# A two-layer hybrid encoder on one core: the residual stream kept with features on partitions, and the output projection turned to match

## The chip, the cores and the metric

The kernel runs on one core of a Trainium2 chip. The metric is the device time of one execution in microseconds; for the kernel before it is 845.27 us, the median of 3 runs (844.89 to 845.55). The profile is that of one execution.

## What is computed

Input x is 256 tokens by 2048 features in float32. Each of two layers normalises x, projects it to all branch inputs, runs four token mixers (retention, gated linear attention, pooling, latent attention), gates them, and adds the output projection to x:

```python
for l in range(DEPTH):                       # DEPTH = 2
    h = _rmsnorm(x, norm_g[l])               # x * rsqrt(mean(x*x) + EPS) * g
    z = h @ w_in[l]
    ...                                      # split z; y_a, y_b, y_c, y_d of the four mixers
    y = jnp.concatenate([y_a, y_b, y_c, y_d], axis=-1)
    x = x + y @ w_out[l]
```

## The kernel before

**Weights as a stream of granules.** All large weights of a layer come as 136 granules of 128 x 1024 float32 (512 KB), two blocks of 128 input rows by 512 output columns each. SyncE loads them into a ring of four buffers `raw` (L319). Each is split in two parts whose sum is the float32 value: ScalarE writes `hi` (L713), VectorE (in each layer POOL for the first three, L1358) writes `lo = raw - hi` (L978). TensorE multiplies hi by hi, lo by hi and hi by lo. The plan is fixed: stage mq has 8 granules (0 to 7), then lat (352 columns wide), and so on to rg (96 to 103) and the output stages out0 to out3 (104 to 135). A buffer is free for `hi` when its granule is `multiplied`, and for `raw` when it is `split`.

**Products.** In every stage of the stream the activations, x or y, are the stationary operand, 128 features by 128 tokens, and the weights are the moving one, 512 columns (L357). A granule is 2 blocks x 2 token halves x 3 products = 12 matmuls. Results go to one of two pairs of PSUM banks, `pair[0]` and `pair[1]`, which alternate from stage to stage; the four others, `bank[0..3]`, serve the mixers. `taken` says that a pair's result has been read. Gates such as rg are read out of their pair by `take` on ScalarE (L731).

**x and its turning.** x lies with tokens on partitions, `x[128, 2, 2048]`. At the start of a layer `turn_x(f)` transposes two feature tiles of x (four 128 x 128 transposes on TensorE, L388) into a bank; ScalarE rounds them with the norm's gain to `xT_hi` (L747) and VectorE writes `xT_lo` (L995). TensorE's order is turn_x(0), turn_x(1), granule 0, turn_x(2), granule 1, and so on. mq alone does the four hi-by-hi products of a granule first, and waits for the low parts behind them. The squares for the norm are taken on ScalarE with a sum over the row (L758); the factor `x_rs` is made by VectorE and POOL and applied when a stage is taken.

**Output.** In out0 to out3, VectorE adds each 128 x 512 result to x (L1325), the first half of the tokens when `half_out` says so, the second when the granule is done. The signals `added[c]` release the next layer's transposes and, in the last layer, SyncE's stores (L324).

**Order.** Every engine's order is written out by hand: `splits(n)` on ScalarE and VectorE and `granules(n)` on TensorE go on to granule n. The body of a layer stands once, in a loop (`Fori`) on each engine, and a wait's number is worked out from the layer register. What VectorE and TensorE do next to the end of a layer is thus the loop's branch back. The first loads are x's first quarter (SyncE), the identity, the gains and x's second quarter (ScalarE), and, after POOL's memsets, the last two quarters of x and the constants (L1344, L1346).

Of the kernel before, what the change touches and what calls it, by code (L numbers as in the profile page):

```python
# [17 lines left out]
F32 = mybir.dt.float32  # L18
# [6 lines left out]
P = 128  # L25
# [31 lines left out]
for i_ in range(4):  # L57
# [7 lines left out]
    ("mq", "lat", "mg", "pv", "pg", "gqk", "gv", "gg", "rq", "rk", "rv", "rg", "out0", "out1", "out2", "out3"))}  # L65
# [3 lines left out]
for n_, count_ in ORDER:  # L69
    w_, t_, b_, k_, per_ = STAGES[n_]  # L70
    if n_ not in done_:
        done_[n_], NTH[n_] = 0, used_[PAIR[n_]]
        used_[PAIR[n_]] += 1
# [40 lines left out]
def build(nc, x_in, stream, mats_in, gains_in, consts_in, out):  # L114
    with ExitStack() as ctx:
# [86 lines left out]
        x_sq = stats(MT * 4).rearrange("p (m c) -> p m c", m=MT)  # L202
# [29 lines left out]
        added = [signal(f"added{c}", MT, primed=1) for c in range(4)]  # L232
        gains_ready = signal("gains_ready", 1)
        half_out = signal("half_out", 4)
        act_step = signal("act_step", 4)
        dve_step = signal("dve_step", 24)
        tabs_ready = signal("tabs_ready", 6)
        x_filled, xT_rounded, xT_ready = signal("x_filled", 8), signal("xT_rounded", KT), signal("xT_ready", KT)
        x_squared, x_ms_ready, x_rs_ready = signal("x_squared", 8), signal("x_ms_ready", 1), signal("x_rs_ready", 1)
# [70 lines left out]
        def _(sp):  # L310

            sp.dma_start(x[:, :, 0:512], x_in.rearrange("(m p) (c n) -> c p m n", p=P, c=4)[0]
                         ).then_inc(x_loaded[0].sem, 16)
# [7 lines left out]
            for c in range(4):  # L321
                for m in range(MT):
                    sp.wait_ge(*added[c].at(DEPTH - 1, m + 1))
                    sp.dma_start(out.rearrange("(m p) (c n) -> m c p n", p=P, c=4)[m, c],  # L324
                                 x[:, m, c * 512:(c + 1) * 512]).then_inc(stored.sem, 16)
            sp.wait_ge(stored.sem, 16 * 4 * MT)
# [3 lines left out]
        def _(pe):  # L330
# [5 lines left out]
            with pe.Fori(0, DEPTH) as l:  # L336
                pos = [0]

                def granules(upto):

                    for j in range(pos[0], upto):
                        name, slots = PLAN[j]
                        width, src, base, n_slots, per = STAGES[name]
                        a, r = PAIR[name], j % RING
                        first = slots[0] == base
                        if first:
                            pe.wait_ge(*taken[a].at(l, MT * NTH[name]))
                        if name == "wq0" and first:
                            pe.wait_ge(*lqT_ready.at(l, 4))
# [1146 lines left out]
```

## Time and profile before

| | |
|---|---|
| median of 3 runs | 845.27 us (844.89 to 845.55) |
| profiled execution, first to last instruction (span) | 843.8 us |
| TensorE busy | 829.3 us (98%) |
| VectorE / ScalarE / POOL busy | 464.5 / 428.4 / 50.2 us |
| matmuls of the weight stream | 3 x 768 on x, 3 x 304 on y |
| mean granted TensorE clock | 0.996 |
| data moved | 150.67 MB, 179 GB/s |

The page gives for the profiled execution only its span; the time of a run is taken around the program, and its median is 1.5 us above the span. An engine that is 98% busy sets the time, so the profile is read for TensorE's own instructions, for its idle time and for what ended it. A matmul's recorded duration (0.39 us for 512 columns) is longer than the distance between two starts, because matmuls overlap; the distance is what counts. The granted clock is given as a share of 2.4 GHz.

### The profile page before, as it was taken

The page shows a single profiled execution, that of the slowest core. Times are in us where ns is not written, and L with a number is a line of the kernel's source. Part 1 is how long each engine was busy: PE and PEld are TensorE (multiplying, and loading weights), DVE is VectorE, ACT ScalarE, POOL GpSimd, SP SyncE. Part 2 cuts the span into 40 slices and gives each one's busy share as a digit, 9 for nine tenths or more (in the row PEclk, how much of TensorE's full clock was granted, in tenths as well). Part 3 has the DMA queues.
Part 4 walks back from the last instruction along what each step waited for, and adds up shares of the span by engine and source line. Part 5 has one row for each costly group of instructions (what it writes and reads, how often), then busy time and mean ns, then how long its engine had stood idle before and what let it go on. Part 6 is the DMA issues. An engine that isn't in the chain of part 4 may idle for free.

```text
span 843.8 us, 11480 instructions
## 1 busy us (share of the span) xinstructions
PE 829.3 (98%) x4084; PEld 701.4 (83%) x4084; DVE 464.5 (55%) x611; ACT 428.4 (51%) x616; POOL 50.2 (6%) x44
## 2 busy tenths in 40 slices
PE   6999999999999999999989999999999999999998
PEld 5898888888888888888869888888878888888886
DVE  2554497445375853654445635864653649546542
ACT  4864565456725543433347655663475345444441
POOL 6110000000000101000122000000000010010000
PEclk9999999999999999999989999999999999999999
DMA  8765764533543454565436656644354345546654
GB/s 343 251 230 190 240 215 150 174 125 126 175 150 125 147 178 150 193 206 198 156 117 227 246 186 227 198 150 150 125 175 147 128 147 162 176 139 204 194 186 140
DMA packets 41924, 150.67 MB, mean 179 GB/s; under 512 B 4752, under 2 KB 4880, under 8 KB 41744
## 3 DMA queue, kind: packets, MB, share of 16 engines
q1 hardware_dynamic: 40592, 145.25, 51.5%
q0 software_dynamic: 432, 2.88, 0.8%
q10 hardware_dynamic: 848, 1.83, 0.7%
q8 instruction: 34, 0.56, 0.3%
q14 instruction: 18, 0.15, 0.1%
HBM read 147.85 MB, written 2.10 MB: 178 GB/s over the span
## 4 chain that ended last, share of the span: by engine, by line
PE 96%; ACT 1%; issue 1%; DMA 1%; DVE 1%; SPq 0%; ACTq 0%; DVEq 0%
PE pair L357 84%; PE bank L388 4%; PE bank L637 1%; PE bank L611 1%; PE bank L500 1%; PE bank L679 1%; PE bank L669 1%; PE bank L592 1%; DMA raw<-stream 1%; PE bank L627 0%; PE bank L548 0%; PE bank L570 0%; PE bank L560 0%; ACT gate L731 0%; DVE lo L978 0%
## 5 line engine op out<-in xcount | busy, mean ns | idle before, releaser
L978 DVE TENSOR_TENSOR lo<-raw,hi 128x1024 fp32r<-128x1024 f32 (+3 forms) x266 | 307.3, 1178 | 213.1 <-ACT hi L713 209.2
L713 ACT ACTIVATE hi<-raw 128x1024 fp32r<-128x1024 f32 (+3 forms) x272 | 270.4, 1022 | 155.7 <-PE pair L357 132.5
L357 PE MATMUL pair<-lo,xT_hi 128*128 128x512 f32 (+1 forms) x768 | 296.9, 387 | 2.4 <-DVE xT_lo L995 2.4
L357 PE MATMUL pair<-hi,xT_hi 128*128 128x512 f32 (+1 forms) x768 | 296.0, 396 | 2.9 <-ACT xT_hi L747 2.6
L357 PE MATMUL pair<-hi,xT_lo 128*128 128x512 f32 (+1 forms) x768 | 296.9, 387 | 0.0
L357 PEld LDWEIGHTS pair<-lo,xT_hi 128*128 128x128 f32 x768 | 145.5, 189 | 30.2 <-issue 3.3
L357 PEld LDWEIGHTS pair<-hi,xT_hi 128*128 128x128 f32 x768 | 144.3, 189 | 30.4 <-ACT xT_hi L747 3.3
L357 PEld LDWEIGHTS pair<-hi,xT_lo 128*128 128x128 f32 x768 | 145.2, 189 | 28.5
L357 PE MATMUL pair<-hi,yT_hi 128*128 128x512 f32 (+1 forms) x304 | 116.7, 384 | 0.0
L357 PE MATMUL pair<-hi,yT_lo 128*128 128x512 f32 (+1 forms) x304 | 116.6, 383 | 0.0
L357 PE MATMUL pair<-lo,yT_hi 128*128 128x512 f32 (+1 forms) x304 | 116.5, 383 | 0.0
L357 PEld LDWEIGHTS pair<-lo,yT_hi 128*128 128x128 f32 x304 | 57.1, 188 | 10.8
L357 PEld LDWEIGHTS pair<-hi,yT_hi 128*128 128x128 f32 x304 | 57.1, 188 | 10.7
L357 PEld LDWEIGHTS pair<-hi,yT_lo 128*128 128x128 f32 x304 | 57.1, 188 | 10.6
L731 ACT ACTIVATE work<-pair,stat 128x512 f32<-128x512 f32 (+2 forms) x44 | 26.4, 653 | 47.0 <-PE pair L357 25.6
L1352 POOL TENSOR_TENSOR stat<-stat 128x2 f32<-128x2 f32 (+1 forms) x10 | 19.1, 1911 | 495.9 <-DVE stat L1001 495.9
L747 ACT ACTIVATE yT_hi<-bank,gains 128x256 fp32r<-128x256 f32 x44 | 17.4, 475 | 52.7 <-PE bank L388 52.7
L995 DVE SCALAR_TENSOR_TENSOR yT_lo<-bank,gains,yT_hi 128x256 fp32r<-128x256 f32 x44 | 18.3, 477 | 29.3 <-ACT yT_hi L747 29.3
L1325 DVE TENSOR_TENSOR x<-pair,x 128x512 f32<-128x512 f32 x16 | 11.1, 692 | 28.4 <-PE pair L357 28.4
L995 DVE SCALAR_TENSOR_TENSOR xT_lo<-bank,gains,xT_hi 128x256 fp32r<-128x256 f32 x32 | 13.9, 478 | 19.7 <-ACT xT_hi L747 19.7
L747 ACT ACTIVATE xT_hi<-bank,gains 128x256 fp32r<-128x256 f32 x32 | 13.3, 469 | 16.7 <-PE bank L388 16.7
L1245 DVE TENSOR_REDUCE stat<-work 128x4 f32<-128x512 f32 x8 | 5.5, 686 | 28.3 <-ACT work L931 15.1
(138 smaller groups left out, 519.7 us busy)
## 6 DMA issues: line engine op xcount, KB each, us to landing
raw<-stream SPq DMA_DIRECT2D x272, 512.0 KB, 4.2
out<-x SPq DMA_DIRECT2D x8, 256.0 KB, 5.3
consts<-consts_in POOLq DMA_DIRECT2D x1, 1792.0 KB, 14.9
mats<-mats_in ACTq DMA_DIRECT2D x2, 576.0 KB, 3.5
x<-x_in POOLq DMA_DIRECT2D x2, 512.0 KB, 9.3
x<-x_in SPq DMA_DIRECT2D x1, 512.0 KB, 4.6
x<-x_in ACTq DMA_DIRECT2D x1, 512.0 KB, 9.0
consts<-consts_in ACTq DMA_DIRECT2D x1, 64.0 KB, 4.3
```

The source lines that it names most:

```text
L357: return nc.tensor.matmul(pair[a][m][:, 0:width], x_part[:, slots[i], m * P:(m + 1) * P], w_part[r][:, i * 512:i * 512 + width], start=(sl ...
L388: t = nc.tensor.transpose(bank[b][:, i * P:(i + 1) * P], tile, ident)
L500: mm = nc.tensor.matmul(bank[m][:, h * HD:(h + 1) * HD], probsT[:, h % 2, j, m * P:(m + 1) * P], kv_sb[:, j, h, NOPE:NOPE + HD], start=(h ...
L592: mm = nc.tensor.matmul(bank[(2 + 2 * m + d) % 4][:, f * SEQ:(f + 1) * SEQ], e_neg[:, d, f, m * P:(m + 1) * P], q_heads[:, d, f, m].rearra ...
L611: mm = nc.tensor.matmul(bank[(2 + 2 * m + d) % 4][:, h * HD:(h + 1) * HD], k_dec[:, d, h], v_b[:, m, h * HD:(h + 1) * HD], start=True, sto ...
L713: nc.scalar.activation(cut[0], cut[1], ACT.Copy).then_inc(rounded[r].sem, 1)
L731: nc.scalar.activation(dst(m), pair[a][m][:, 0:cols], func, scale=rs[:, m:m + 1]).then_inc(ready.sem, 1)
L747: nc.scalar.activation(dst[:, slot0 + kt, :], bank[(b0 + f) % 4][:, i * SEQ:(i + 1) * SEQ], ACT.Copy, scale=gains[:, gain + kt:gain + kt + ...
L978: nc.vector.tensor_tensor(cut[0], cut[1], cut[2].bitcast(F32), ALU.subtract).then_inc(split[r].sem, 1)
L995: nc.vector.scalar_tensor_tensor(out=dst_lo[:, slot0 + kt, :], in0=bank[(b0 + f) % 4][:, i * SEQ:(i + 1) * SEQ], scalar=gains[:, gain + kt ...
L1325: nc.vector.tensor_tensor(at, pair[PAIR[f"out{c}"]][m][:], at, ALU.add).then_inc(added[c].sem, 1)
L1352: pool.tensor_tensor(rs, ms, minus_half[:, 0:n], ALU.pow).then_inc(rs_ready.sem, 1)
```

## The change

- x enters, stays and leaves with features on partitions, `xT[128, 16, 256]`; the host turns it. The transposes of x (`turn_x`) are gone. ScalarE makes xT_hi and VectorE xT_lo straight from xT in SBUF.
- In out0 to out3 the weights become the stationary operand, four tiles of 128 output columns per block, and y the moving one. y's high and low parts lie side by side in `yT[:, slot]` (2 x 256), so that one matmul of 512 columns gives weights-hi by y-hi and by y-lo, in the two halves of a bank; a second of 256 columns adds weights-lo by y-hi to the first half. Each output quarter uses four banks: the two pairs for out0 and out2, `bank[0..3]` for out1 and out3.
- VectorE adds both halves to xT, two dependent adds of 256 columns per tile. Before the adds of the last quarter of the first layer it makes the next layer's first eight tiles of xT_lo.
- The squares for the norm are now summed over partitions: ScalarE squares 1024 columns at a time into gate0 and gate1, POOL folds them into `x_sum[128, 256]`, and TensorE multiplies x_sum by a column of -0.5 ahead of mq's last granule.
- The loop over layers is written out on all engines but SyncE. POOL issues its x loads ahead of the memsets; ScalarE loads gains, x's second quarter and then the identity.

```diff
--- before.py
+++ after.py
-        yT_hi = sb("yT_hi", [P, KT, SEQ], F32R)
-        yT_lo = sb("yT_lo", [P, KT, SEQ], F32R)
-        x = sb("x", [P, MT, D_MODEL])
+        yT = sb("yT", [P, KT, 2, SEQ], F32R)
+        yT_hi, yT_lo = yT[:, :, 0, :], yT[:, :, 1, :]
+        xT = sb("xT", [P, KT, SEQ])
+        x_sum = sb("x_sum", [P, SEQ])
...
-            with pe.Fori(0, DEPTH) as l:
+            for l in range(DEPTH):
...
+                def out_granule(j, c, slots, first):
+                    r = j % RING
+                    pe.wait_ge(*split[r].at(l, j // RING + 1))
+                    if c == 0 and slots[0] % GT == 0:
+                        pe.wait_ge(*(yTD_ready, yTC_ready, yTB_ready, yTA_ready)[slots[0] // GT].at(l, 4))
+                    for t in range(4):
+                        into = pair[t // 2][t % 2] if c % 2 == 0 else bank[t]
+                        if first and c == 0 and t % 2 == 0:
+                            pe.wait_ge(*taken[t // 2].at(l, MT * PAIR_USES[t // 2]))
...
+                        if first and c >= 2:
+                            pe.wait_ge(*added.at(l, 4 * (c - 2) + t + 1))
+                        for i, slot in enumerate(slots):
+                            at = slice(i * 512 + t * P, i * 512 + (t + 1) * P)
+                            nc.tensor.matmul(into[:], hi[r][:, at], yT[:, slot].rearrange("p a t -> p (a t)"),
+                                             start=slot == 0, stop=False)
+                            mm = nc.tensor.matmul(into[:, 0:SEQ], lo[r][:, at], yT[:, slot, 0, :],
+                                                  start=False, stop=slot == KT - 1)
+                        if slots[-1] == KT - 1 and t < 3:
+                            mm.then_inc(tile_out.sem, 1)
+                    mm.then_inc(multiplied[r].sem, 1)
...
-                for f in range(8):
...
-                    turn_x(f)
-                    if f >= 1:
-                        granules(f)
+                granules(7)
+                pe.wait_ge(*x_summed.at(l, 4))
+                pe.wait_ge(*added.at(l, 0))
+                pe.wait_ge(cleared.sem, 1)
+                for m in range(MT):
+                    mm = nc.tensor.matmul(bank[2][:, 2 * m:2 * m + 2], x_sum[:, m * P:(m + 1) * P], minus_half[:, 0:2],
+                                          start=True, stop=True)
+                mm.then_inc(ms_filled.sem, 1)
                 granules(13)
...
+                def lo_x(l, f):
+                    dve.wait_ge(*xT_rounded.at(l, 2 * f + 2))
+                    for kt in (2 * f, 2 * f + 1):
+                        nc.vector.scalar_tensor_tensor(
+                            out=xT_lo[:, kt, :], in0=xT[:, kt, :], scalar=gains[:, G_NORM + kt:G_NORM + kt + 1],
+                            in1=xT_hi[:, kt, :].bitcast(F32), op0=ALU.mult, op1=ALU.subtract).then_inc(xT_ready.sem, 1)
...
                 for c in range(4):
                     splits(min(114 + 8 * c, GRANULES))
-                    j = END[f"out{c}"] - 1
-                    dve.wait_ge(*half_out.at(l, c + 1))
-                    for m in range(MT):
...
+                    if c == 3 and l + 1 < DEPTH:
+                        for f in range(4):
+                            lo_x(l + 1, f)
+                    for t in range(4):
...
+                        nc.vector.tensor_tensor(at, into[:, 0:SEQ], at, ALU.add).then_inc(half_added.sem, 1)
+                        dve.wait_ge(*half_added.at(l, 4 * c + t + 1))
+                        nc.vector.tensor_tensor(at, into[:, SEQ:2 * SEQ], at, ALU.add).then_inc(added.sem, 1)
...
+            for c in range(2, 4):
+                pool.dma_start(xT[:, 4 * c:4 * c + 4, :], x_in[c]).then_inc(x_loaded[c].sem, 16)
             pool.memset(minus_half, -0.5).then_inc(cleared.sem, 1)
...
+                for c in range(4):
+                    sq = (gate0, gate1)[c % 2][:].rearrange("p m c -> p (m c)")
+                    pool.wait_ge(*x_squared.at(l, c + 1))
+                    pool.tensor_tensor(sq[:, 0:512], sq[:, 0:512], sq[:, 512:1024], ALU.add).then_inc(x_folded.sem, 1)
...
```

**TensorE at the start of a layer.** The rows name the line, the operation, the tile written and those read, and the waits. Before:

```order
L406 ISA [waits x_loaded0,yA_ready]
L388 MATMUL bank<-consts,x 128x128 [waits added0]
L388 MATMUL bank<-consts,x 128x128 x7
L347 ISA
L365 ISA [waits taken0]
L366 ISA [waits rounded0]
L357 MATMUL pair<-hi,xT_hi 128x512 [waits xT_rounded]
L357 MATMUL pair<-hi,xT_hi 128x512 x3
L370 REGISTER_ALU [waits xT_ready]
L357 MATMUL pair<-lo,xT_hi 128x512 [waits split0]
```

After, from the last two matmuls of the first layer on:

```order
L363 MATMUL bank<-yT,hi 128x512
L365 MATMUL bank<-yT,lo 128x256
L392 MATMUL pair<-hi,xT_hi 128x512 [waits rounded0,xT_rounded,added,taken0]
L392 MATMUL pair<-hi,xT_hi 128x512 x3
L392 MATMUL pair<-lo,xT_hi 128x512 [waits split0,xT_ready]
```

The eight transposes between out3 and mq are gone, with the waits of the turned tiles, and mq follows out3 directly.

**TensorE in the first output granule.** Before:

```order
L370 REGISTER_ALU [waits yTD_ready,taken0]
L357 MATMUL pair<-hi,yT_hi 128x512 [waits split0]
L357 MATMUL pair<-lo,yT_hi 128x512
L357 MATMUL pair<-hi,yT_lo 128x512
L357 MATMUL pair<-hi,yT_hi 128x512
L357 MATMUL pair<-lo,yT_hi 128x512
```

After:

```order
L363 MATMUL pair<-yT,hi 128x512 [waits taken0,yTD_ready,split0]
L365 MATMUL pair<-yT,lo 128x256
L363 MATMUL pair<-yT,hi 128x512
L365 MATMUL pair<-yT,lo 128x256
L363 MATMUL pair<-yT,hi 128x512
L365 MATMUL pair<-yT,lo 128x256
L363 MATMUL pair<-yT,hi 128x512
L365 MATMUL pair<-yT,lo 128x256
L363 MATMUL pair<-yT,hi 128x512 [waits taken1]
```

Wide and narrow matmuls alternate, and from the third tile on the granule needs the second pair of banks too, which before was not needed until out1.

**VectorE at the last output quarter of the first layer.** Before:

```order
L978 TENSOR_TENSOR lo<-raw,hi 128x1024 [waits rounded3]
L1325 TENSOR_TENSOR x<-pair,x 128x512 [waits half_out]
L1323 REGISTER_ALU
L1325 TENSOR_TENSOR x<-pair,x 128x512 [waits multiplied3]
L968 REGISTER_ALU [waits added3]
L968 COMPARE_AND_BRANCH
```

After:

```order
L1004 TENSOR_TENSOR lo<-raw,hi 128x1024 [waits rounded3]
L1033 SCALAR_TENSOR_TENSOR xT_lo<-xT,gains,xT_hi 128x256 [waits xT_rounded]
L1033 SCALAR_TENSOR_TENSOR xT_lo<-xT,gains,xT_hi 128x256
...
L1367 TENSOR_TENSOR xT<-bank,xT 128x256 [waits tile_out]
L1369 TENSOR_TENSOR xT<-bank,xT 128x256 [waits half_added]
...
L1367 TENSOR_TENSOR xT<-bank,xT 128x256 [waits multiplied3]
L1369 TENSOR_TENSOR xT<-bank,xT 128x256 [waits half_added]
L1004 TENSOR_TENSOR lo<-raw,hi 128x1024 [waits rounded3,gains_ready]
```

The next layer's first xT_lo tiles stand ahead of the adds, and its first split of VectorE behind them.

## Rows read from the trace of the kernel before

**Rows 1.** The page's head and busy times of the engines.
```profile
span 843.8 us, 11480 instructions
PE 829.3 (98%) x4084; PEld 701.4 (83%) x4084; DVE 464.5 (55%) x611; ACT 428.4 (51%) x616; POOL 50.2 (6%) x44
```
**Rows 2.** Waits of TensorE: whom it waited for, us in total, times, longest.
```profile
PE bank L388 <- DMA x<-x_in: 5.6, 1, 5.6
PE pair L357 <- ACT xT_hi L747: 2.6, 2, 2.1
PE pair L357 <- DVE xT_lo L995: 2.4, 1, 2.4
```
**Rows 3.** Timeline of TensorE, change of layers: start, us, operation, idle before.
```profile
422.05 0.39 PE L357 MATMUL pair<-hi,yT_lo 128*128 128x512 f32 x1
...
423.96 1.19 PE L357 MATMUL pair<-hi,xT_hi 128*128 128x512 f32 x4 [0.49 <-ACT xT_hi L747]
427.51 0.79 PE L357 MATMUL pair<-lo,xT_hi 128*128 128x512 f32 x1 [2.36 <-DVE xT_lo L995]
...
454.24 0.32 PE L357 MATMUL pair<-hi,xT_hi 128*128 128x352 f32 x1
```
**Rows 4.** ScalarE and VectorE there; last, a window's busy times, clock, DMA share, GB/s.
```profile
423.07 0.84 ACT L747 ACTIVATE xT_hi<-bank,gains 128x256 fp32r<-128x256 f32 x2 [5.13 <-PE bank L388]
426.50 1.66 DVE L995 SCALAR_TENSOR_TENSOR xT_lo<-bank,gains,xT_hi 128x256 fp32r<-128x256 f32 x4 [3.33 <-ACT xT_hi L747]
427.50:433.00 5.50, 5.49 (x15) 4.42 (x16) 0.66 (x2) 0.82 (x3) 2.11 (x1) 0.50 0.56 191
```
**Rows 5.** Timeline of TensorE at the start of the first layer.
```profile
14.49 0.60 PE L388 MATMUL bank<-consts,x 128*128 128x128 f32 x4
14.84 1.17 PE L357 MATMUL pair<-hi,xT_hi 128*128 128x512 f32 x4
...
33.70 1.07 PE L357 MATMUL pair<-hi,xT_hi 128*128 128x512 f32 x4
36.42 0.32 PE L357 MATMUL pair<-hi,xT_hi 128*128 128x352 f32 x1
```
**Rows 6.** POOL and ScalarE at the start, and a window with its DMA rate.
```profile
4.03 1.67 POOL L1344 DMA_DIRECT2D x<-x_in x2
7.87 1.06 ACT L713 ACTIVATE hi<-raw 128x1024 fp32r<-128x1024 f32 x1 [3.78 <-DMA raw<-stream]
9.01 2.36 POOL L1358 TENSOR_TENSOR lo<-raw,hi 128x1024 fp32r<-128x1024 f32 x1 [2.74 <-ACT hi L713]
6.00:8.00 2.00, 1.58 (x8) 1.17 (x6) 0.00 (x0) 0.13 (x1) 0.27 (x1) 1.00 1.01 359
```
**Rows 7.** TensorE in the attention scores and out stage, and the page's weight loads.
```profile
138.54 0.28 PE L472 MATMUL bank<-yT_lo,yT_hi 128*128 128x256 f32 x1
140.10 0.28 PE L477 MATMUL bank<-yT_lo,yT_hi 128*128 128x256 f32 x1
391.90 0.39 PE L357 MATMUL pair<-lo,yT_hi 128*128 128x512 f32 x1
398.70 0.39 PE L357 MATMUL pair<-lo,yT_hi 128*128 128x512 f32 x1
L357 PEld LDWEIGHTS pair<-lo,yT_hi 128*128 128x128 f32 x304 | 57.1, 188 | 10.8
```
**Rows 8.** Timeline of TensorE and ScalarE where out0 begins.
```profile
334.33 0.39 PE L357 MATMUL pair<-hi,yT_hi 128*128 128x512 f32 x1
334.53 1.27 ACT L731 ACTIVATE gate<-pair,stat 128x512 f32<-128x512 f32 x2 [2.97 <-PE pair L357]
```
**Rows 9.** End of the program, and VectorE's cost for 256 columns from PSUM.
```profile
839.91 0.39 PE L357 MATMUL pair<-hi,yT_lo 128*128 128x512 f32 x1
840.34 0.69 DVE L1325 TENSOR_TENSOR x<-pair,x 128x512 f32<-128x512 f32 x1 [0.67 <-PE pair L357]
L995 DVE SCALAR_TENSOR_TENSOR xT_lo<-bank,gains,xT_hi 128x256 fp32r<-128x256 f32 x32 | 13.9, 478 | 19.7 <-ACT xT_hi L747 19.7
```

More of the change, by code:

```diff
@@ L64 @@
 PAIR = {n_: i_ % 2 for i_, n_ in enumerate(
[L65 removed]
+    ("mq", "lat", "mg", "pv", "pg", "gqk", "gv", "gg", "rq", "rk", "rv", "rg"))}
 PAIR.update({n_: 0 for n_ in ("wq0", "wq1", "wkv0", "wkv1")})
@@ L321, in _ @@
             for c in range(4):
-                for m in range(MT):
[L323 to L326, printed above, removed]
+                sp.wait_ge(*added.at(DEPTH - 1, 4 * c + (4 if c < 3 else 1)))
+                n = 4 if c < 3 else 1
+                sp.dma_start(out[c, :, 0:n], xT[:, 4 * c:4 * c + n, :]).then_inc(stored.sem, 16)
+            for j in range(1, 4):
+                sp.wait_ge(*added.at(DEPTH - 1, KT - 4 + j + 1))
+                sp.dma_start(out[3, :, j:j + 1], xT[:, KT - 4 + j:KT - 3 + j, :]).then_inc(stored.sem, 16)
+            sp.wait_ge(stored.sem, 16 * 7)
         @block.tensor
@@ L343, in granules @@
                         width, src, base, n_slots, per = STAGES[name]
+                        first = slots[0] == base
+                        if name.startswith("out"):
+                            out_granule(j, int(name[3:]), slots, first)
+                            continue
                         a, r = PAIR[name], j % RING
-                        first = slots[0] == base
                         if first:
                             pe.wait_ge(*taken[a].at(l, MT * NTH[name]))
+                        if first and name in ("mq", "lat"):
+                            pe.wait_ge(*added.at(l, (10 if name == "mq" else 12) - KT))
                         if name == "wq0" and first:
@@ L371, in granules @@
                         ends = slots[-1] == base + n_slots - 1
-                        if name.startswith("out") and ends:
-                            each.sort(key=lambda im: im[1])
                         for i, m in each:
@@ L378, in granules @@
                             mm = product(i, m, t_lo, hi, last=ends and i == per - 1)
-                            if name.startswith("out") and ends and (i, m) == (per - 1, 0):
-                                mm.then_inc(half_out.sem, 1)
                         mm.then_inc(multiplied[r].sem, 1)
@@ L962, in _ @@
         def _(dve):
-            for sig in (*split, *added, yA_ready, yTA_ready, la_ready, score_b_ready):
+            for sig in (*split, yA_ready, yTA_ready, la_ready, score_b_ready):
                 dve.sem_inc(sig.sem, 1)
+            dve.sem_inc(added.sem, KT)
             dve.wait_ge(gains_loaded.sem, 16)
             nc.vector.tensor_copy(gains[:], gains_all[:, 0:GAIN_W]).then_inc(gains_ready.sem, 1)
-            with dve.Fori(0, DEPTH) as l:
+            for l in range(DEPTH):
                 pos, step = [POOL_SPLITS], [0]
```

136 lines of the change are left out of this document (68 added, 68 removed).

## The prediction

> **What bounds the kernel now.** I read the page's busy shares first: TensorE is busy 829.3 of a span of 843.8 us, VectorE and ScalarE about half of it [rows 1]. So only what TensorE executes, and what it waits for, counts. Its waits come to under 11 us, and all of the long ones are in the stretch in which x is turned and rounded: 5.6 for the first part of x, 2.6 for xT_hi, 2.4 for xT_lo [rows 2]. The timeline then says where. At the change of layers the last output matmul is issued at 422.05, the transposes follow, TensorE waits 0.49 for ScalarE, does four matmuls, waits 2.36 for VectorE, and the stage behind (lat, the first of 352 columns) begins only at 454.24 [rows 3]. VectorE's idle time of 3.33 us ends long after its input is there (xT_hi is written from 423.07 on, 0.84 us for both tiles; VectorE starts at 426.50; I take this for the branch back of its loop, since nothing else stands there), and after TensorE's wait the granted clock is 0.50, the lower of its two levels (1.2 of 2.4 GHz) [rows 4]. Everything else is a steady stream: in the output stage 30 matmuls of 512 columns start in 6.80 us, 226.7 ns each [rows 7]. The sum below is made against the profiled span of 843.8 us; the median of the runs, 845.27 us, is 1.5 above it, and I carry the difference over unchanged.
>
> **Out stage, more matmuls: +3.4 us.** A granule was 12 matmuls of 512 columns, 12 x 0.2267 = 2.72 us. It becomes 8 of 512 and 8 of 256: the same 6144 columns, but four more instructions and weight loads. The only 256-column matmuls of the same data type stand in the attention scores: 13 intervals in 1.56 us, 120 ns each, every one with its own weight load [rows 7]. 8 x 0.2267 + 8 x 0.120 = 2.774, so +0.053 per granule, and 64 granules give +3.4. Lower end: two narrow ones cost what a wide one did, 113 ns each, so nothing is added: 0. What the row doesn't show is a narrow matmul between wide ones; that is a rival below. The Trainium skill (TensorE: Matmul & The Clock Gate, section "Packing small matmuls", what overlaps) says that a weight load overlaps a running matmul only in another row group, and gives a load of 128 columns as 107 ns ("LDWEIGHTS"). By that rule this change's 4 x 64 = 256 extra loads would add 27 us instead of 3.4. A whole 256-column matmul with its load stands every 120 ns, so the trace speaks against it.
>
> **Change of layers: -9.9 us.** Before, from the end of the last output matmul (422.05 + 0.23 = 422.28) to the first lat matmul (454.24) pass 31.96 us [rows 3]. In that stretch lie 8 granules of mq, 8 x 2.72 = 21.8; the rest is 32 transposes, the waits and matmuls at half clock. After the change the transposes are gone, the loop is written out, and mq's first six granules need features 0 to 1535, whose sums are complete one quarter earlier; VectorE makes the low parts of the first eight feature tiles before it adds the last quarter. Tiles 12 to 15 are needed 6 x 2.72 = 16 us after the last output matmul, and their 8 adds take 4 us. What is late next is the norm: squares on ScalarE, three folds per quarter on POOL, then a matmul ahead of mq's last granule (19 us after). POOL takes 2.36 us for 1024 columns [rows 6], so one quarter's folds of 512, 256 and 256 are 2.4 us; ScalarE's last square waits behind a split that needs granule 3 multiplied (11 us), so the sum is there at 11 + 1.1 + 1.1 + 2.4 + latencies, some 16 us: hidden, with 3 to spare. The two matmuls of 2 columns themselves I put at 0.3 us (4 transposes take 14.84 - 14.49 = 0.35 us [rows 5]; ends 0.2 and 0.6). 31.96 - 21.8 - 0.3 = 9.9 saved, ends 9.3 and 10.1.
>
> **Start: -0.5 us, the least certain term.** Before, the first lat matmul is at 36.42. Granule 0 is done when the transposes at 14.49 begin, and mq's last granule, 7, starts at 33.70: 19.2 us for six granules, which need 6 x 2.72 = 16.3. So the six sets of transposes between them cost 2.9 [rows 5]. Granule 0 itself is bound by its low part: weights landed and ScalarE at 7.87, POOL from 9.01 to 11.37 [rows 6], which no transpose delays. So the best case is -2.9 + 0.3 = -2.6. Against it stands the order of loads. POOL now issues its two x transfers (1 MB) ahead of its memsets instead of at 4.03 [rows 6], and ident, for which TensorE waits at its very start, is queued on ScalarE behind 0.5 MB of x. The DMA engines are full there, 359 GB/s from 6 to 8 us [rows 6], so 1 MB ahead of the first weights is up to 2.8 us. Then POOL's three splits of 2.4 us follow one another, and only VectorE's, from granule 3 on, catch up; the end of this case is +1.5. I take half of the delay, so most of the gain is spent: -0.5. The Trainium skill (DMA: Bandwidth & Descriptors, "Queues, rings and completion order", arbitration) says that each engine goes round its queues packet by packet. By it the weights would get a third while three queues have work, and the first granule would land about 2 us later; that would put this term near zero.
>
> **Handover of rg: +0.7 us.** The first output granule now writes all four pair banks. Two of them hold rg, which ScalarE takes from 334.53 to 335.80 and releases near 336.05; the granule starts at 334.33 [rows 8] and reaches the third tile after 8 of 16 matmuls, 1.39 us later, at 335.72. So TensorE waits 0.35 in each layer, 0.7 in all (ends 0 and 1.0).
>
> **End: +1.1 us.** Before, VectorE's last add (0.69) starts at 840.34, 0.2 after the last matmul's slot (839.91 + 0.23) [rows 9]. Now each 128x256 tile is two chained adds. The nearest row is 0.48 for 256 columns out of PSUM [rows 9]; half the 512-wide add is 0.35; I take 0.43. A tile with its waits is near 1 us, TensorE makes one in 0.69, so VectorE falls behind and ends 2.0 after the last matmul instead of 0.9: +1.1, ends 0.7 and 2.0. The same backlog stands at the other quarters: VectorE is 2 us late with the next split, which is due 5.5 us after the quarter's end, so it costs nothing; if it did, TensorE would show waits on lo in each quarter.
>
> The unrolled loop adds no instruction that is executed and removes register work; outside the change of layers the rows show no cost for it, so zero. The new load order of yT and the adds of lo_x out of SBUF lie on ScalarE and VectorE, half idle: zero.
>
> **Sum:** 3.4 - 9.9 - 0.5 + 0.7 + 1.1 = -5.2, so 845.27 - 5.2 = 840.1 us.
>
> **Rivals.**
> 1. *The narrow matmul exposes its weight load* (slower). A weight load is recorded with 188 ns [rows 7]. If a narrow matmul behind a wide one held TensorE for its load's 188 instead of 120, 512 x 0.068 = 35 us: 875 us. There are 512 narrow matmuls, so the gain of 5.2 is gone from 130 ns each, and from 134 on it is slower by over 0.2%. For it: no row has this mixture. Against: 120 ns in the scores. The Trainium skill's rule on weight loads (TensorE: Matmul & The Clock Gate, as above) points the same way as this rival, with less. 8%.
> 2. *The sum of squares comes late.* If POOL's folds or their semaphores take twice what I say, TensorE waits about 2 us in each layer ahead of granule 7: 844 us. Against it: 3 us of slack at the change of layers; for it, about 1 us at the start. 8%.
> 3. *The start is fast:* the loads keep their order of arrival, -2.6 instead of -0.5, and VectorE's adds cost what half a wide one does: 837.6. 15%.
> 4. *The low clock stays.* A new wait at the start or at the layers keeps TensorE at the lower level for some 6 us, as after 427.51; 3 us are given back: 843. 6%.
> 5. *The adds at each quarter starve the ring,* 1 us in each of 6 quarters: 846, no difference. 5%.
>
> **Numbers.** My forecast, 839 to 842, has 58%. The range takes in rivals 2 to 4: 836.6 to 844.0; outside are rivals 1 and 5 and a little of the fast side. A measurement of this kernel can tell 0.2%, 1.7 us, from nothing. Faster: the forecast, 3, 4 and a part of 2, about 0.82; within 0.2%: rival 5 and the rest of 2, 0.10; slower: rival 1, 0.08.
>
> **What would show it.** The output stage at 2.77 us per granule, narrow matmuls every 120 ns. From the last output matmul of the first layer to the first lat matmul 22.1 us, no wait of TensorE over 0.3 there, granted clock at the upper level throughout, no transposes of x. A wait near 0.35 for ScalarE in the first output granule. The first lat matmul at 36 and the last add some 2 us behind TensorE's last. I am wrong if narrow matmuls stand 130 ns apart or more, if TensorE waits for x_sum, or if the first lat matmul comes after 38.

## The result, and the profile after

The changed kernel takes 846.03 us (median of 20 runs, 845.78 to 846.35); the kernel before, on the same chip, 844.92 (20 runs; one of them, at 1045.8 us, was slow and is left out of the ratio). The ratio is 1.0017, with a 95% interval of 1.0010 to 1.0024. Forecast were 840.1 and a range of 836.6 to 844.0, so the prediction was wrong: about 5 us of gain were expected, and 1.1 us of loss came.

The page of the changed kernel, its head and the busy rows, and VectorE's row of xT_lo:

```profile
span 844.4 us, 11528 instructions
PE 824.6 (98%) x4284; PEld 705.0 (83%) x4284; DVE 499.5 (59%) x657; ACT 425.0 (50%) x590; POOL 75.0 (9%) x66
...
L1033 DVE SCALAR_TENSOR_TENSOR xT_lo<-xT,gains,xT_hi 128x256 fp32r<-128x256 f32 x32 | 32.9, 1069 | 11.0 <-ACT xT_hi L776 11.0
```

TensorE is busy 4.7 us less than before [rows 1], in a span that is 0.6 longer, so it waits more. And one instruction of VectorE, same shape, has gone from 478 [rows 9] to 1069 ns. The waits of TensorE after the change (whom it waited for, us in total, times, longest):

```profile
PE pair L392 <- ACT hi L733: 10.9, 1, 10.9
PE pair L392 <- DVE lo L1004: 3.7, 5, 1.0
PE pair L392 <- POOL lo L1397: 1.1, 2, 0.8
```

The waits for xT_hi and xT_lo [rows 2] are gone. In their place stand a longer start and waits of 1 us for lo, the low part of the weights. The timeline of TensorE says where (start, us, operation, idle before):

```profile
10.95 2.05 PE L392 MATMUL pair<-hi,xT_hi 128*128 128x512 f32 x4 [10.95 <-ACT hi L733]
...
30.38 1.07 PE L392 MATMUL pair<-hi,xT_hi 128*128 128x512 f32 x4
32.48 0.47 PE L392 MATMUL pair<-lo,xT_hi 128*128 128x512 f32 x1 [1.03 <-DVE lo L1004]
34.38 1.07 PE L392 MATMUL pair<-hi,xT_hi 128*128 128x512 f32 x4
...
41.61 0.32 PE L392 MATMUL pair<-hi,xT_hi 128*128 128x352 f32 x1
...
429.49 0.28 PE L365 MATMUL bank<-yT,lo 128*128 128x256 f32 x1
429.60 1.09 PE L392 MATMUL pair<-hi,xT_hi 128*128 128x512 f32 x4
...
449.57 0.50 PE L428 MATMUL bank<-stat,x_sum 128*128 128x2 f32 x4
...
452.78 0.32 PE L392 MATMUL pair<-hi,xT_hi 128*128 128x352 f32 x1
```

The first lat matmul comes at 41.61 instead of 36.42 [rows 5]. The granules of mq follow one another every 4.0 us (30.38 to 34.38) where 2.72 was reckoned. The change of layers, in contrast, is nearly a stream without a wait (the longest is 0.2 us): out3's last matmul is issued at 429.49, lat begins 23.29 us later, where 32.19 passed before [rows 3].

Four points in time divide the span of every kernel of this study: the first matmul of out0 in layer 1, the issue of the last output matmul of layer 1, the first lat matmul of layer 2, and the end of the span. All are read from TensorE's timeline:

```
kernel                        start to out0   out stage   to lat of layer 2   rest     span
before                            334.33        87.72           32.19        389.56   843.8
after                             339.38        90.11           23.29        391.62   844.4
  difference                       +5.05        +2.39           -8.90         +2.06    +0.6
before, loop written out          333.83        87.72           26.70        389.15   837.4
```

The last line is the fourth experiment's. It shows what the prediction had not separated: 5.5 of the 8.9 us at the change of layers are got without the change of layout. The +2.06 of the rest is the second layer's out stage, 90.10 us (750.55 to 840.65) where 87.72 passed before, less 0.3 in other places.

VectorE in the first layer after the change:

```profile
6.65 0.88 DVE L1033 SCALAR_TENSOR_TENSOR xT_lo<-xT,gains,xT_hi 128x256 fp32r<-128x256 f32 x2 [1.05 <-ACT xT_hi L776]
11.49 2.36 DVE L1033 SCALAR_TENSOR_TENSOR xT_lo<-xT,gains,xT_hi 128x256 fp32r<-128x256 f32 x2 [3.96 <-ACT xT_hi L776]
...
30.58 1.76 DVE L1004 TENSOR_TENSOR lo<-raw,hi 128x1024 fp32r<-128x1024 f32 x1
32.26 2.39 DVE L1033 SCALAR_TENSOR_TENSOR xT_lo<-xT,gains,xT_hi 128x256 fp32r<-128x256 f32 x2
34.57 1.75 DVE L1004 TENSOR_TENSOR lo<-raw,hi 128x1024 fp32r<-128x1024 f32 x1
36.25 0.87 DVE L1033 SCALAR_TENSOR_TENSOR xT_lo<-xT,gains,xT_hi 128x256 fp32r<-128x256 f32 x2
```

VectorE at the change of layers, after:

```profile
426.21 7.04 DVE L1033 SCALAR_TENSOR_TENSOR xT_lo<-xT,gains,xT_hi 128x256 fp32r<-128x256 f32 x4 [0.37 <-ACT xT_hi L776]
```

And POOL in the first layer:

```profile
10.81 2.37 POOL L1397 TENSOR_TENSOR lo<-raw,hi 128x1024 fp32r<-128x1024 f32 x1 [4.40 <-ACT hi L733]
...
20.89 1.48 POOL L1402 TENSOR_TENSOR gate<-gate 128x512 f32<-128x512 f32 x1
...
31.21 2.27 POOL L1402 TENSOR_TENSOR gate<-gate 128x512 f32<-128x512 f32 x1
33.56 0.81 POOL L1407 TENSOR_TENSOR gate<-gate 128x256 f32<-128x256 f32 x1
34.45 0.79 POOL L1411 TENSOR_TENSOR x_sum<-x_sum,gate 128x256 f32<-128x256 f32 x1
```

Two xT_lo tiles take 0.88 us while POOL is idle (6.65; 36.25, just after its last fold of x at 35.24) and about 2.4 while it splits or folds; a split of VectorE takes 1.75 instead of the 1.23 it had before. POOL's fold of 512 columns takes 1.48 beside xT_lo (20.89) and 2.27 where a split of VectorE runs with it (31.21); POOL's own splits keep 2.4 us beside xT_lo. One mq granule needs one split and two xT_lo from VectorE, 1.76 + 2.39 less some overlap: the 4.0 us of TensorE's granules.

ScalarE's first two roundings show the second cause, the loads:

```profile
9.60 1.06 ACT L733 ACTIVATE hi<-raw 128x1024 fp32r<-128x1024 f32 x1 [3.06 <-DMA raw<-stream]
...
13.58 1.06 ACT L733 ACTIVATE hi<-raw 128x1024 fp32r<-128x1024 f32 x1 [2.12 <-DMA raw<-stream]
```

Before, the first weights were there at 7.87 [rows 6]. So two theories stood after this reading, for the +5.05: A, the order of the first loads delays the weights; B, VectorE and POOL slow each other down, now that VectorE reads xT_lo's operands, x and xT_hi, both from SBUF, where it used to read x from PSUM.

### The profile page after: what moved, and what is told of

Same layout as the page of the kernel before. It is cut to its first block, busy times and chain, and to the rows that moved or that the text cites. A ratio compares the mean times of both kernels' runs of the same rounds, so it can differ in the third digit from the quotient of the medians.

```text
span 844.4 us, 11528 instructions
## 1 busy us (share of the span) xinstructions
PE 824.6 (98%) x4284; PEld 705.0 (83%) x4284; DVE 499.5 (59%) x657; ACT 425.0 (50%) x590; POOL 75.0 (9%) x66
## 4 chain that ended last, share of the span: by engine, by line
PE 91%; DVE 5%; DMA 2%; ACT 1%; issue 1%; SPq 0%; ACTq 0%
PE pair L392 59%; PE pair L363 7%; PE bank L363 6%; PE pair L365 3%; PE bank L365 3%; PE bank L419 3%; DVE xT_lo L1033 3%; DVE lo L1004 2%; DMA raw<-stream 2%; PE bank L658 1%; PE bank L632 1%; PE bank L700 1%; PE bank L521 1%; PE bank L613 1%; PE bank L690 1%
## 5 line engine op out<-in xcount | busy, mean ns | idle before, releaser
L363 PE MATMUL pair<-yT,hi 128*128 128x512 f32 x256 | 90.0, 395 | 0.1
L363 PE MATMUL bank<-yT,hi 128*128 128x512 f32 x256 | 88.9, 391 | 0.0
L365 PE MATMUL pair<-yT,lo 128*128 128x256 f32 x256 | 71.7, 280 | 0.0
L365 PE MATMUL bank<-yT,lo 128*128 128x256 f32 x256 | 71.7, 280 | 0.0
L363 PEld LDWEIGHTS pair<-yT,hi 128*128 128x128 f32 x256 | 48.0, 187 | 11.6 <-ACTq L756 0.8
L363 PEld LDWEIGHTS bank<-yT,hi 128*128 128x128 f32 x256 | 47.9, 187 | 10.5
L365 PEld LDWEIGHTS pair<-yT,lo 128*128 128x128 f32 x256 | 48.4, 189 | 0.1
L365 PEld LDWEIGHTS bank<-yT,lo 128*128 128x128 f32 x256 | 48.4, 189 | 0.0
L1033 DVE SCALAR_TENSOR_TENSOR xT_lo<-xT,gains,xT_hi 128x256 fp32r<-128x256 f32 x32 | 32.9, 1069 | 11.0 <-ACT xT_hi L776 11.0
L392 PE MATMUL pair<-hi,yT 128*128 128x384 f32 (+1 forms) x96 | 27.5, 353 | 0.0
```

The source lines that it names most:

```text
L363: nc.tensor.matmul(into[:], hi[r][:, at], yT[:, slot].rearrange("p a t -> p (a t)"), start=slot == 0, stop=False)
L365: mm = nc.tensor.matmul(into[:, 0:SEQ], lo[r][:, at], yT[:, slot, 0, :], start=False, stop=slot == KT - 1)
L392: return nc.tensor.matmul(pair[a][m][:, 0:width], x_part[:, slots[i], m * P:(m + 1) * P], w_part[r][:, i * 512:i * 512 + width], start=(sl ...
L1033: nc.vector.scalar_tensor_tensor(out=xT_lo[:, kt, :], in0=xT[:, kt, :], scalar=gains[:, G_NORM + kt:G_NORM + kt + 1], in1=xT_hi[:, kt, :]. ...
```

## The experiments

Every kernel ran beside the kernel before on the same chip; the ratios are to it.

### 1 to 3: the loads, the folds, and both

In e1 the first loads are issued in the order of before:

```diff
 act:
+    act.dma_start(const("ident"), consts_in[:, 0:P])
     act.dma_start(gains_all[:], gains_in)
     act.dma_start(xT[:, 4:8, :], x_in[1])
-    act.dma_start(const("ident"), consts_in[:, 0:P])
 pool:   (the two x loads)
-    ahead of the memsets
+    behind the memsets
```

In e2 POOL's folds of the squares shrink to two columns each, so most of the mean square of x is left out:

```diff
-pool.tensor_tensor(sq[:, 0:512], sq[:, 0:512], sq[:, 512:1024], ALU.add)
+pool.tensor_tensor(sq[:, 0:2], sq[:, 0:2], sq[:, 512:514], ALU.add)
```

(the other folds in the same way, but for the first of 256 columns in each layer). e3 has both edits.

Expected of e1:

> The changed kernel with the first loads issued as before (POOL's x loads behind its memsets, ScalarE: identity, gains, x). Theory A, the loads alone made the start late (weights of granule 0 landed at 9.6 instead of 7.9 us): the first lat matmul comes back from 41.6 to about 36, the time falls by 5 us to 841. Theory B, VectorE's xT_lo out of SBUF (two operands in SBUF, 1.2 us instead of 0.44 while POOL folds the squares) made it late: the time falls by 1 us at most. I expect both to count: first lat matmul near 39.5, 844 us.

Of e2:

> The changed kernel with POOL's folds cut to 2 columns (only one 256-column add per layer is kept), so the norm's sum leaves out most of the squares. Theory A (loads): start unchanged, 846. Theory B (POOL beside VectorE): xT_lo tiles behind granule 2 take 0.44 us each again, the splits 1.23 instead of 1.76; the first lat matmul comes near 38.5, 843 us; the 3 tiles made beside POOL's own splits stay slow.

Of e3:

> Both edits: loads issued as before, and POOL's folds cut to 2 columns (the norm's sum leaves out most squares). If A and B are all of it, the start is as the prediction had it: first lat matmul at 34.5 to 36, 839.5 to 841 us. If it stays above 38, something else holds the start.

Measured: e1 842.95 us (ratio 0.9978, 0.9969 to 0.9988), e2 840.73 (0.9951, 0.9935 to 0.9968), e3 839.41 (0.9933, 0.9917 to 0.9950). Out0 starts at 335.12, 334.73 and 333.66, where it was 339.38. In e2, VectorE shows what an idle POOL does. Rows of its timeline:

```profile
11.00 2.35 DVE L1033 SCALAR_TENSOR_TENSOR xT_lo<-xT,gains,xT_hi 128x256 fp32r<-128x256 f32 x2 [3.48 <-ACT xT_hi L776]
...
23.05 0.87 DVE L1033 SCALAR_TENSOR_TENSOR xT_lo<-xT,gains,xT_hi 128x256 fp32r<-128x256 f32 x2
23.84 1.21 DVE L1004 TENSOR_TENSOR lo<-raw,hi 128x1024 fp32r<-128x1024 f32 x1
```

Beside POOL's splits (11.00) the pair still takes 2.35; once the splits are over, 0.87, and the split of VectorE 1.21. And in e1, where the weights come early, VectorE meets POOL's three splits and the first folds in one stretch:

```profile
9.14 10.79 DVE L1033 SCALAR_TENSOR_TENSOR xT_lo<-xT,gains,xT_hi 128x256 fp32r<-128x256 f32 x6 [2.08 <-ACT xT_hi L776]
```

Six xT_lo take 10.79 us, 1.8 each, for which 0.44 each would do. Both theories hold, each for a part, and the parts are not independent: e1 gets 3.1 us back, e2 5.3, both together 6.6. So the folds are worth 3.5 us (from e1 to e3) to 5.3, the loads 1.3 (from e2 to e3) to 3.1. Both were larger than I had expected of the single edits: the first lat matmul comes at 37.30 in e1 and 36.93 in e2, where I had 39.5 and 38.5; in e3 it comes at 35.85, as expected. With both edits, out0 starts 0.67 us before that of the kernel before, close to what the prediction had for this term (-0.5), but with most of the norm's folds left out. How large the loads' part is stays rough: ScalarE's first rounding in the profiled executions is at 7.25 in e1, but at 8.96 in e3, which has the same loads, and at 9.11 in e2, which has the late ones.

### 4: the kernel before with its loop over the layers written out

```diff
-            with pe.Fori(0, DEPTH) as l:
+            for l in range(DEPTH):
```

The same on ScalarE, VectorE and POOL, in the kernel before; nothing else.

> The kernel before with the loop over layers written out on TensorE, ScalarE, VectorE and POOL, nothing else. Theory: the loop's branch kept VectorE from starting (3.33 us idle) and led to the 2.36 us wait of TensorE and to 6 us at half clock; without it some 5 us fall away at the change of layers, 840 us. Rival: the wait belongs to the chain transposes, xT_hi, xT_lo, and stays; 844.5 us or more.

Measured: 839.52 us (839.48 to 839.56), ratio 0.9937 (0.9920 to 0.9953), span 837.4. The kernel before took 844.75 beside it, so this edit alone brings 5.2 us, as much as was forecast for the whole change. VectorE of this kernel at the change of layers:

```profile
423.42 0.88 DVE L995 SCALAR_TENSOR_TENSOR xT_lo<-bank,gains,xT_hi 128x256 fp32r<-128x256 f32 x2 [0.75 <-ACT xT_hi L747]
```

It starts 0.94 after ScalarE's first xT_hi (422.48), and no longer 3.43 after it, as before [rows 4]. TensorE no longer waits for xT_lo, and in the window in which its granted clock was 0.50, the lower level, it now has the full one (window, us; then busy times with counts of PE, PEld, DVE, ACT, POOL; clock, DMA share, GB/s):

```profile
427.50:433.00 5.50, 5.50 (x29) 4.53 (x28) 3.18 (x5) 4.09 (x9) 1.61 (x1) 1.00 0.72 229
```

29 matmul records in 5.5 us where there were 15 [rows 4]. From the last output matmul to lat pass 26.70 instead of 32.19. Two parts make up the 5.49: TensorE goes from the first four hi-by-hi products to the first low part 2.55 us sooner (1.00 after 423.46, where it was 3.55 after 423.96), and from there to the first low part of the next granule pass 3.22 us instead of the 6.14 (427.51 to 433.65) in which its matmuls stood 0.43 us apart. One run of the kernel before, among the 17 beside e10, bears this out: it alone has a mean granted clock of 1.000, and it takes 842.24 us where the others take 844.1 to 846.0. The Trainium skill (Runtime: NRT & Kernel Launch, "Instruction fetch mechanics") says that a taken branch whose target lies outside the instruction window forces a fetch before the engine goes on. VectorE's idle time of 3.33 us [rows 4] and its fall to 0.75 here agree with that; that it is the fetch is not shown by any run.

Against this kernel, and not against the one before, the change of layout costs 7.0 us of span: +5.55 to out0, +2.39 in the out stage, -3.41 at the change of layers, +2.47 behind.

### 5 and 6: can the start be repaired?

e5 has e1's loads and puts the first layer's squares and folds behind the xT_lo work, and with them the small matmul that sums them:

```diff
-                    if f in (2, 3, 5, 7):
-                        square_x((2, 3, 5, 7).index(f))
+                    if l and f in (2, 3, 5, 7):
+                        square_x((2, 3, 5, 7).index(f))
+                    if not l and f in (6, 7):
+                        square_x(f - 6)
...
-                granules(7)
+                granules(7 if l else 11)
```

(squares 2 and 3 follow still later, and the splits ahead of the small matmul's result go on to granule 14). e6 adds to it that VectorE makes POOL's three splits of layer 1 itself:

```diff
-                for j in range(POOL_SPLITS):
+                for j in range(POOL_SPLITS if l else 0):
```

> The changed kernel, complete, with the first loads issued as before and, in the first layer only, the squares and POOL's folds moved behind VectorE's xT_lo work (squares at feature pairs 6 and 7 and behind granules 8 and 9, the sum's matmul ahead of granule 11). If POOL beside VectorE was the second cause of the late start, it is gone without leaving anything out: first lat matmul near 36, 840 us. If the order of the norm's chain matters in another way, TensorE waits ahead of granule 11 or of the turning of zq, and the time stays near 843.

> As e5, and in the first layer VectorE takes POOL's three splits too. With POOL idle all of VectorE's operations out of SBUF should run at their short times (0.44 and 1.23 us) and granule 0's low part comes 1.2 us earlier: 838.5 to 839.5. If POOL's splits were no burden, nothing changes against e5 (840).

Measured: e5 841.20 us (0.9946, 0.9932 to 0.9959; its five runs lie from 839.60 to 841.41), e6 840.11 (0.9940, 0.9925 to 0.9956). Nothing is left out in either. e5 takes 1.7 us less than e1 with the same loads, and 1.2 more than expected; its TensorE waits 1.4 us for x_sum. With VectorE idle, POOL's fold takes 1.28 (e5's timeline of POOL):

```profile
37.66 1.28 POOL L1408 TENSOR_TENSOR gate<-gate 128x512 f32<-128x512 f32 x1
```
In e6 VectorE's pairs stay at 0.88 until the first fold, though it does more work:

```profile
8.35 1.23 DVE L1010 TENSOR_TENSOR lo<-raw,hi 128x1024 fp32r<-128x1024 f32 x1 [1.00 <-ACT hi L733]
9.49 0.88 DVE L1039 SCALAR_TENSOR_TENSOR xT_lo<-xT,gains,xT_hi 128x256 fp32r<-128x256 f32 x2
...
25.91 2.16 DVE L1039 SCALAR_TENSOR_TENSOR xT_lo<-xT,gains,xT_hi 128x256 fp32r<-128x256 f32 x2 [0.16 <-ACT xT_hi L776]
```

The last pair, beside the first fold, takes 2.16. Out0 starts at 333.42, earlier than in any other kernel of the study. What is left of waits is new, and of my making (TensorE's waits, same kernel):

```profile
PE bank L428 <- POOL x_sum L1418: 2.1, 1, 2.1
```

It is enough to account for e6 being 0.6 above what I had expected at most. e6 stays 0.6 behind e4, within what their intervals leave open.

### 7: the change's order of loads in the kernel before

The reverse of e1's edit, made in the kernel before.

> The kernel before with the changed kernel's order of first loads (POOL's x ahead of the memsets; gains, x, identity on ScalarE), nothing else. Here VectorE reads x's parts from PSUM, so only the loads can act. If they were worth what e1 gave back (3 us), the time is 847 to 848 and granule 0's weights land after 9 us; if e1's gain came mostly from an early run of luck in landing, within 1 us of 844.8.

Measured: 848.08 us, ratio 1.0038 (1.0024 to 1.0051), span 846.3: 3.1 us slower than the kernel before beside it, as expected. In its profile out0 starts 4.0 us later (338.35), and the change of layers is 1.5 shorter (30.72). Its TensorE waits

```profile
PE bank L388 <- DMA consts<-consts_in: 11.5, 1, 11.5
```

for ident, which its transposes need and which now stands last in ScalarE's queue. ScalarE rounds the first weights at 10.61 instead of 7.87. The first of these two is a cost that the changed kernel doesn't have; the second it has (9.60). So e7 shows that the order of loads costs time in the old layout too, but not how much of it the changed kernel pays.

### 8: useless adds on POOL in the kernel before with its loop written out

This is the test of what exactly collides. Eight adds of 128x512 out of SBUF that nothing uses, per layer, behind POOL's splits:

```diff
+                for i in range(8):
+                    pool.tensor_tensor(gate1[:, i % 2, :], k_dec[:, 0], k_dec[:, 1], ALU.add)
```

(reshaping and semaphores left out here). VectorE here reads xT_lo's x from PSUM, and lo's operands from SBUF.

> The kernel before, unrolled (e4, 839.5 us), with eight useless adds of 128x512 on POOL behind its splits in each layer, beside VectorE's xT_lo from PSUM and splits from SBUF. Theory: POOL and VectorE get in each other's way only where VectorE reads both operands from SBUF: the splits beside an add take 1.76 instead of 1.23 us, xT_lo stays at 0.44, and the time rises by less than 1 us. Rival: any VectorE operation suffers, xT_lo goes to 1 us too, and the time rises by 2 or more.

Measured: 841.07 us (0.9949, 0.9934 to 0.9965), 1.5 above e4. The operations, first VectorE's timeline, then POOL's:

```profile
22.48 2.31 DVE L979 TENSOR_TENSOR lo<-raw,hi 128x1024 fp32r<-128x1024 f32 x1 [1.23 <-ACT hi L714]
24.71 0.86 DVE L996 SCALAR_TENSOR_TENSOR xT_lo<-bank,gains,xT_hi 128x256 fp32r<-128x256 f32 x2
25.49 1.52 DVE L979 TENSOR_TENSOR lo<-raw,hi 128x1024 fp32r<-128x1024 f32 x1
...
32.08 1.23 DVE L979 TENSOR_TENSOR lo<-raw,hi 128x1024 fp32r<-128x1024 f32 x1 [0.67 <-ACT hi L714]
```

```profile
16.06 13.48 POOL L1362 TENSOR_TENSOR gate<-k_dec 128x512 f32<-128x512 f32 x8
```

This settles what collides in B. Beside the adds (16.06 to 29.54) the split with two SBUF operands takes 1.5 to 2.3 us instead of 1.23; the xT_lo with one operand in PSUM stays at 0.43 each. The same instruction of VectorE is slowed in the changed kernel because its x now lies in SBUF. The Trainium skill (GPSIMD Engine Reference, "Specifications") says that POOL shares its SBUF interfaces with VectorE, and names instructions of VectorE with two SBUF inputs as one of two kinds that contend. These rows agree: 1.5 to 2.3 us with two inputs in SBUF, 0.43 with one.

In the profiled execution the 1.5 us are not the adds'. They arise ahead of the first add (16.06). In both kernels the first matmuls on weights, from 9.8 on, start 0.43 us apart, the distance that they had at the change of layers under a granted clock of 0.50, though the clock column reads 1.00 here. In e4 this ends at 12.98, in e8 only at about 16. The same matmul in e4, then in e8:

```profile
12.98 0.40 PE L357 MATMUL pair<-hi,xT_lo 128*128 128x512 f32 x1
12.98 0.63 PE L358 MATMUL pair<-hi,xT_lo 128*128 128x512 f32 x1
```

So the transposes that e4 starts at 14.13 and 17.34 start at 15.12 and 18.80 here, and from then on granules follow every 3.20 us in both kernels. The weights were there at the same time (ScalarE's first rounding at 7.84 and 7.85). In e10 below, the same kernel as e4 in another execution, the slow stretch lasts until 14.4, and out0 starts 0.82 later than in e4 (334.65 against 333.83). Its length varies between executions, and so does the landing of the first loads: with the old order in the changed kernel ScalarE first rounds at 7.25 (e1), 8.96 (e3), 8.29 (e5), 7.26 (e6) and 8.75 (e9). A difference of 1 to 1.5 us at the start of one profiled execution tells nothing. Whether the adds cost something in e8's other runs (840.04 to 841.22 in all, e10's 839.24 to 840.43) stays open.

### 9 and 10: an attempt at the best form, and e4 again

e9 is e6 with the small matmul one granule later (12) and the query transposes behind two more granules, and with ScalarE's and VectorE's splits ahead of them going on to granule 15; e10 is e4's kernel again, on the same chip.

```diff
-                granules(7 if l else 11)
+                granules(7 if l else 12)
...
-                granules(13)
+                granules(13 if l else 15)
```

> The changed kernel with all start-up repairs (old load order, first layer's squares and folds behind the attention-query products, VectorE taking POOL's three weight splits of layer 1) and, new here, the small matmul that sums the squares placed one granule later and the query transposes two granules later in layer 1. If the last wait of TensorE on the POOL sums (2.1 us in the run before this one) is only a matter of place, the time falls by 1 to 2 us from 840.1, to 838.3 to 839.1, just under the 839.5 of the kernel before with its loop written out. Rival: the wait moves on to the transposes of the query latents, which need the same sums by way of POOL, VectorE and ScalarE; then 840.0 stays within 0.4.

> The kernel before with its loop over the layers written out, once more, to stand on the same chip beside the best form of the change: 839.5 within 0.5 again. If it comes out above the other run by more than 0.5 us, the residual stream with features on partitions is worth having once its start is repaired; if equal or below, the whole change brings nothing that writing out the loop does not bring alone.

Measured: e9 844.62 us (0.9995, 0.9987 to 1.0004), e10 839.83 (0.9941, 0.9928 to 0.9953). e9 is a failure of the kind that its text did not name. The wait for x_sum is gone, but TensorE now waits

```profile
52.97 0.43 PE L392 MATMUL pair<-hi,xT_hi 128*128 128x352 f32 x1 [3.26 <-DVE lo L1010]
```

3.26 us for a weight split: the transposes come at 48.68, ScalarE and VectorE round the query latents behind them, and the next splits are queued behind that on both engines. Behind this wait the granted clock falls (window, columns as above):

```profile
53.00:56.00 3.00, 3.00 (x12) 3.00 (x13) 2.19 (x2) 0.46 (x1) 0.00 (x0) 0.59 0.61 205
56.00:59.00 3.00, 3.00 (x13) 2.51 (x12) 0.00 (x0) 2.36 (x11) 0.00 (x0) 0.84 0.87 280
```

Six microseconds at a mean of 0.72 instead of 1.00 are 1.7 lost on top of the 3.26. That is the price the prediction's rival 4 spoke of, in another place. The rest of e9's distance to e6 (out0 at 338.05 against 333.42) lies at the start: the first lat matmul is at 34.73 instead of 32.48, with the loads issued in the same order: ScalarE's first rounding is at 8.75 instead of 7.26, and the first matmuls stand 0.43 apart for 0.8 us longer. 2.1 for x_sum are saved. That sums to 3.3 + 1.7 + 2.2 - 2.1 = 5.1 for 4.6 seen. e10 repeats e4 within 0.3 us. e4's edit is the best form found: it beats both the kernel before and the changed one, and no complete form of the new layout beat it; whether e6 equals it is not settled, since the two did not run on the same chip.

## Why the prediction was wrong, step by step

- **"The new load order of yT and the adds of lo_x out of SBUF lie on ScalarE and VectorE, half idle: zero"**: this is the step that failed. I put the xT_lo out of SBUF at nothing, by VectorE's mean load over the span; what I had measured was the same operation out of PSUM, 0.478. Out of SBUF beside POOL it costs 1.2, VectorE's split 1.76 instead of 1.23, and in the first layer POOL is busy almost without a pause from 18.53 to 35.24, with its last split and the change's own folds. VectorE then paces TensorE at 4.0 us per granule. The step was wrong in kind: neither a rival nor the range had it. A second size was wrong beside it: I had put a quarter's folds at 2.4 us, by columns; they take 4.0 (31.21 to 35.24), and 3.1 at the change of layers, so POOL is in VectorE's way for longer than the prediction would have had it.
- **Start, -0.5.** Measured +5.05 to out0. By e2 and e3, the folds' contention is the larger part. The trace agrees: the first product on weights is only 1.2 us later than before (10.95 against 9.71), the other 4 come from the distance of the granules behind it. The order of loads I had named, with +1.5 as its worst end; undoing it gave 3.1 us of time in e1, and 1.3 with the folds gone. So the end of +1.5 may have been too small even for the part that I saw. The identity, which I had queued behind 0.5 MB of x, costs nothing: no wait of TensorE ends with it. The sentence that it would be wrong "if the first lat matmul comes after 38" is the one that came true, at 41.61.
- **Change of layers, -9.9.** Measured -8.9 (-8.8 when counted from the last matmul's slot, as in the prediction): nearly right in size, even though four xT_lo take 7 us there (426.21). Most of the difference of 1 lies with POOL beside VectorE: with the folds cut to two columns (e2) the stretch is 22.41 instead of 23.29. But whose gain it is, I had not separated: e4 shows 5.5 of it for the loop alone, which I had read correctly as a branch and then booked in one term with the transposes. The layout's own part is 3.4.
- **Out stage, +3.4, and handover, +0.7.** Measured +2.39 in the first layer and +2.38 in the second, for which my terms give 1.7 + 0.35 each. In the steady part a wide and a narrow matmul together take what I summed (68 pairs in 23.57 us from 400.14 on, 346.6 ns each); about 0.25 more is in out0, whose pairs stand some 353 ns apart. Rows of TensorE in the first output granule after:

```profile
340.67 0.28 PE L365 MATMUL pair<-yT,lo 128*128 128x256 f32 x1
341.02 0.50 PE L363 MATMUL pair<-yT,hi 128*128 128x512 f32 x1
341.36 0.28 PE L365 MATMUL pair<-yT,lo 128*128 128x256 f32 x1
...
429.14 0.28 PE L365 MATMUL bank<-yT,lo 128*128 128x256 f32 x1
429.25 0.39 PE L363 MATMUL bank<-yT,hi 128*128 128x512 f32 x1
429.49 0.28 PE L365 MATMUL bank<-yT,lo 128*128 128x256 f32 x1
```

  From narrow to narrow 0.35 at 429.14, as 0.2267 + 0.120 gives. From 340.67 to 341.36 it is 0.69, and this is the handover of rg: 0.34, for which I had 0.35. Rival 1, the exposed weight load, is refuted: it needed 188 ns where 120 stand. The rule of the Trainium skill (TensorE: Matmul & The Clock Gate, "Packing small matmuls") that a weight load overlaps only with matmuls of another row group does not hold for these rows either; the measurement decides.
- **End, +1.1.** Measured -0.1. The last matmul of the program starts at 840.65 and the last add at 841.72 (timeline of the end):

```profile
840.65 0.28 PE L365 MATMUL bank<-yT,lo 128*128 128x256 f32 x1
...
841.72 0.42 DVE L1369 TENSOR_TENSOR xT<-bank,xT 128x256 f32<-128x256 f32 x1
```

  From the last matmul's end (840.77) to the last add's (842.14) pass 1.37 us, before 0.89 by [rows 9]: half of what I had reckoned, since a tile's two adds take 0.79 and not 1. From there the span ends 2.3 us later instead of 2.8; the last transfer is 128 KB instead of 256, which may be why. So the span ends 3.6 to 3.7 behind the last matmul in both.
- **Rivals 2, 4 and 5** did not come: TensorE doesn't wait for x_sum, the page's clock row shows no dip (the slow distance of the first matmuls is there in the kernel before too), and none of the listed waits lies at the quarters. Rival 3's start would have put out0 some 2 us earlier than before; only e6 comes near (0.9 earlier), and it needed three more edits.

Sum of the measured: 5.05 + 2.39 - 8.90 + 2.06 = +0.6 of span; the medians say +1.1. Apart from the start, every term of the sum came within 1.2 us of what I had put down; the loss of the forecast gain is the start's.

What stays open: whether the changed kernel with a loop would have been slower by the same 5.5 us. Its layers differ in code, so it wasn't tried; the share of the loop rests on e4. e4 shows that the loops written out take 2.5 us off VectorE's wait at the change of layers; why a branch costs that is not shown.

## What to carry to other kernels

Cost an operation with its operands where they will lie and beside the engines that run then: a VectorE instruction that moves from PSUM to SBUF, and reads two SBUF operands, is exposed to POOL, and a share of busy time says nothing of it. When a change does two things, reckon each alone; the cheap one (here a loop written out) may hold all of the gain. What is issued ahead of the first weights can delay them: by 1.7 us in the profile here (9.60 against 7.87), by 2.7 in e7.

## What the runs showed of the hardware

- VectorE and POOL out of SBUF at once, float32: scalar_tensor_tensor 128x256 goes from 0.44 to 1.2 us, tensor_tensor 128x1024 from 1.23 to 1.76 (1.5 to 2.31 in e8). POOL's tensor_tensor 128x512 takes 1.28 with VectorE idle (e5), 1.48 beside xT_lo and up to 2.27 beside a split of VectorE; its 128x1024 takes 2.4 alone or beside xT_lo. With one of VectorE's operands in PSUM: 0.43, no effect (e8).
- The branches back of the loops cost 5.5 us at one change of layers: VectorE started 3.43 us behind its input instead of 0.94, and TensorE's granted clock behind the wait was 0.50 for 5.5 us, and without it 1.00.
- Wide and narrow matmuls in turn, each with its own weight load of 128 columns, run at 346.6 ns a pair: the loads of 188 ns by the record are hidden even behind 256 columns.
- The first matmuls on weights start 0.43 us apart instead of 0.23, while the clock column reads 1.00. In e4 this lasts until 12.98, in e8 until about 16, though TensorE did the same at the same times up to 12.98.
